# A decoder step with a 32-expert mixture on one core: entry, start and end reordered, expert gates turned by whole-array transposes

## What is computed

```python
x = x + gt1 * _rmsnorm(merged @ w_out, g_post_mix)
h2 = _rmsnorm(x, g_pre_ffn) * (1.0 + sc2) + sh2
logits = h2 @ w_router + b_router            # 32 experts
top_val, top_idx = lax.top_k(logits, 4); gates = softmax(top_val)
# for each expert e: y += gate * swiglu(xb @ w_gate_up[e] + b) @ w_down[e] + b
x = x + gt2 * _rmsnorm(y, g_post_ffn)
```

## Time and profile before

| | before |
|---|---|
| median of 3 runs | 1269.04 us (1268.74 to 1273.98) |
| the profiled execution | 1268.32 us, span 1266.6 us |
| mean granted TensorE clock | 0.946 |
| PE busy | 1087.7 us (86%) |
| DVE busy | 597.7 us (47%) |
| ACT busy | 224.9 us (18%) |
| HBM traffic | 486.16 MB by DMA, mean 384 GB/s |

### The profile page before, as it was taken

How to read it: one execution, slowest core, us unless ns; L and a number is a source line. 1 busy time by engine, 2 the same in 40 slices (tenths; PEclk the granted TensorE clock), 3 DMA queues, 4 the chain that set the end, 5 groups by cost and what they waited for, 6 DMA issues and landing times.

```text
span 1266.6 us, 23750 instructions
## 1 busy us (share of the span) xinstructions
PE 1087.7 (86%) x9790; PEld 462.8 (37%) x9790; DVE 597.7 (47%) x1126; ACT 224.9 (18%) x371; POOL 60.0 (5%) x106
## 2 busy tenths in 40 slices
PE   6999999999888796995788978999866996667996
PEld 3776777784422131331222322333211331112332
DVE  3537744344654352553353643666432552333654
ACT  3002410132311110111011111211111111101112
POOL 0312020310200000000000000000000000000000
PEclk9999999999889898998897999999987998889999
DMA  9979894696899999999999999999999999999996
GB/s 344 306 246 355 316 331 144 212 352 267 321 416 427 428 429 428 428 428 428 428 428 428 426 428 410 394 422 428 428 427 429 427 428 427 428 427 429 428 428 246
DMA packets 67282, 486.16 MB, mean 384 GB/s; under 512 B 6013, under 2 KB 28882, under 8 KB 40426
## 3 DMA queue, kind: packets, MB, share of 16 engines
q1 hardware_dynamic: 59584, 462.11, 88.2%
q0 software_dynamic: 6496, 19.48, 4.7%
q10 hardware_dynamic: 1130, 3.50, 0.8%
HBM read 479.31 MB, written 5.77 MB: 383 GB/s over the span
## 4 chain that ended last, share of the span: by engine, by line
DMA 45%; PE 26%; DVE 1%; issue 0%; ACT 0%; DVEq 0%; ACTq 0%
DMA big<-in_w_down 28%; PE PB L1147 13%; DMA big<-in_w_gate_up 12%; PE PB L1174 7%; DMA hTG<-in_w_down 5%; PE PB L1108 2%; PE PB L1116 2%; PE PB L1132 1%; PE PB L1123 1%; PE PB L1140 0%; PE PB L1093 0%; DVE big L1476 0%; DVE cst L1473 0%; DVE big L1473 0%; ACT L1419 0%
## 5 line engine op out<-in xcount | busy, mean ns | idle before, releaser
L1147 PE MATMUL PB<-big,cst 128*32 128x512 f32 x2768 | 354.3, 655 | 109.5 <-DMA big<-in_w_gate_up 109.5
L2057 DVE TENSOR_TENSOR tok<-PB,cst 32x512 f32<-32x512 f32 x188 | 129.1, 687 | 257.9 <-ACT cst L1418 255.9
L1147 PEld LDWEIGHTS PB<-big,cst 128*32 128x32 f32 x2768 | 88.7, 115 | 346.3 <-issue 182.6
L1174 PE MATMUL PB<-big,cst 128*32 128x512 f32 x1408 | 165.0, 597 | 20.9 <-DMA big<-in_w_down 20.9
L719 PE MATMUL PB<-hTG,big 128*128 128x264 f32 x576 | 138.1, 394 | 1.5 <-DVE hTG L1470 1.5
L2034 DVE TENSOR_SCALAR mod<-PB 64x512 f32<-64x512 f32 x48 | 33.3, 693 | 208.0 <-PE PB L1147 207.9
L719 PEld LDWEIGHTS PB<-hTG,big 128*128 128x128 f32 x576 | 107.8, 192 | 28.9 <-issue 11.8
L1413 ACT ACTIVATE mod<-PB 64x512 f32<-64x512 f32 x48 | 28.4, 592 | 420.4 <-PE PB L1147 420.4
L1108 PE MATMUL PB<-wide,att 128*32 128x256 f32 x1176 | 80.3, 406 | 5.5 <-DVE att L2029 5.5
L1174 PEld LDWEIGHTS PB<-big,cst 128*32 128x32 f32 x1408 | 38.9, 109 | 104.4 <-issue 64.9
L1108 PEld LDWEIGHTS PB<-wide,att 128*32 128x32 f32 x1176 | 39.7, 115 | 61.0 <-issue 36.7
(11 more groups left out here) (346 smaller groups left out, 909.2 us busy)
## 6 DMA issues: line engine op xcount, KB each, us to landing
big<-in_w_gate_up SPq DMA_DIRECT2D x115, 2048.0 KB, 30.9
big<-in_w_down SPq DMA_DIRECT2D x57, 2048.0 KB, 23.7
hTG<-in_w_gate_up SPq DMA_DIRECT2D x13, 2048.0 KB, 38.6
big<-in_w_mod SPq DMA_DIRECT2D x24, 1024.0 KB, 7.6
big<-in_w_in SPq DMA_DIRECT2D x22, 1024.0 KB, 9.0
hTG<-in_w_down SPq DMA_DIRECT2D x6, 2048.0 KB, 24.1
wide<-in_cache_k POOLq DMA_DIRECT2D x16, 256.0 KB, 5.9
big<-in_w_out SPq DMA_DIRECT2D x4, 1024.0 KB, 10.1
```

Source lines behind the costliest of these rows:

```text
L1147: mm = pe.matmul(GU[32 * j:32 * j + 32, :], mo["xT"][:, (2 * u + r) * M:(2 * u + r + 1) * M], groups(w[:, r * 2 * D:(r + 1) * 2 * D])[:, j ...
L1174: mm = pe.matmul(DN[32 * j:32 * j + 32, :], mo["actT"][:, (4 * u + r) * M:(4 * u + r + 1) * M], w[:, r * D + half * 512:r * D + (half + 1) ...
L2057: mm = dve.tensor_tensor(mo["y"][rows, :], DN[rows, :], mo["y_part"][other, :], ALU.add)
```

## The change

1. **Start.** The three loads at the head of SP's queue go to the head of ACT's, so that SP begins with `x_prompt`. Pieces of the shift weights are loaded between the two halves of the first `w_in` unit. PE gets extra matmuls on zeros (`warm`) into a bank that is overwritten, and the order of `x_T`, `scale_part(3)` and `mt0` changes; DVE scales the first seven of eight `hT` chunks before the last is there.
2. **Entry.** `G` and `hT` change places in `hTG`. Units 6 and 9 are loaded in halves: 6's right half right after unit 7, 9's left half after the first half of the last residual. For that the sample rows of `x` are read again by POOL into `xn[:, 1, :]`. The last chunk's scaling is split round the last routing on DVE, POOL's two adds wait for `xT_ready`, and `gather` adds the shift rows itself for the first block. PE gets extra matmuls (`spare`) between steps.
3. **Gates.** `Pg` is written four times side by side by the same reduce, whose input now has a broadcast dimension (128x384 out), and `gates_T` is three whole-array transposes.
4. **End.** The last block is taken out of ACT's loop, so that the Sqrt table is loaded before the last copy. The scatter is done in eight matmuls of 32 rows with a wait after four, prompt before samples; the squares, roots and gains follow that order; chunk 1's rows are scaled and stored in two halves. All four small stores are on SP.

```diff
-AUX_ORDER = ["vt"] + [f"xt{k}" for k in range(KC)] + """
-    mt0 shm mtS ...
+AUX_ORDER = ["vt"] + [f"xt{k}" for k in range(KC - 1)] + ["mt0", f"xt{KC - 1}"] + """
+    shm mtS ...
-        hT = hTG[:, 0:KC * T].rearrange("p (k t) -> p k t", k=KC)
+        hT = hTG[:, 2 * D:2 * D + KC * T].rearrange("p (k t) -> p k t", k=KC)
-        G = hTG[:, KC * T:KC * T + 2 * D].rearrange("p (s n) -> p s n", s=2)
+        G = hTG[:, 0:2 * D].rearrange("p (s n) -> p s n", s=2)
-        mo["Pg"] = cst[:, dead + 512:dead + 608]
+        mo["Pg"] = cst[:, dead + 512:dead + 896]
+        xs_again = xn[:, 1, :]
@@ SP
+            def load_half(n, r):
+                u = n % NU
+                rows = a["w_gate_up"][0, n // NU, u * 2 * P:(u + 1) * 2 * P, :].rearrange("(p r) n -> p r n", r=2)
+                sp.dma_start(unit_slot(n)[:, r * 2 * D:(r + 1) * 2 * D], rows[:, r, :]).then_inc(unit_landed(n)[0], 16)
-            for dst, src in ((vrows[VC:VC + 8, :], a["c_prompt"]...), (vrows[VC + 8:VC + 72, :], a["c_sample"]...),
-                             (cst[:, 0:P + E], a["consts"][:, 0:P + E])):
-                sp.dma_start(dst, src).then_inc(S("small_loaded"), 16)
-                if u == ("in", FIRST, 1):
-                    for i in range(4):
+                if u[0] == "in" and u[1] == FIRST:
+                    for i in range(2 * u[2], 2 * u[2] + 2):
                         sp.dma_start(sh_pieces[:, i, :, :], ...)
             load_unit(7)
+            load_half(6, 1)
             sp.wait_ge(S("wo_half_used"), 1)
             load_unit(4)
             sp.wait_ge(S("yo_full"), 4)
             load_unit(5)
+            sp.wait_ge(S("x1_half"), 2 * NCH - 1)
+            load_half(9, 0)
             sp.wait_ge(S("x_spilled"), 32)
             sp.wait_ge(S("x1_half"), 2 * NCH)
             sp.wait_ge(S("aux_full"), AUX["xa1"] + 1)
-            load_unit(6)
+            load_half(6, 0)
             sp.wait_ge(S("aux_full"), AUX["rt1"] + 1)
-            load_unit(9)
+            load_half(9, 1)
@@ POOL
+            pool.wait_ge(S("aux_full"), AUX["so"] + 1)
+            pool.dma_start(xs_again[0:NS, :], a["x_sample"][:, 0, :]).then_inc(S("ffn_loaded"), 16)
             pool.wait_ge(S("h2_ready"), NCH)
+            pool.wait_ge(S("xT_ready"), 1)
             for lo, hi, row in ffn_shift:
                 pool.tensor_tensor(xn[:, 1, lo:hi], xn[:, 1, lo:hi], row, ALU.add).then_inc(S("h2_ready"), 1)
@@ PE
+            def warm(n):
+                flat = SH1p.rearrange("p k r -> p (k r)")
+                for _ in range(n):
+                    pe.matmul(PB[0][:, 0:256], flat[:, 0:P], flat[:, :], start=True, stop=True)
+            pe.wait_ge(S("zeros_ready"), 1)
+            warm(4)
+            warm(6)
             scale_part(0)
+            warm(3)
             scale_part(1)
             for k in range(4):
                 x_T(k)
             scale_part(2)
-            for k in range(4, KC):
+            for k in range(4, 6):
                 x_T(k)
             scale_part(3)
+            x_T(6)
+            warm(1)
             first_cols("mt0", 1)
+            x_T(7)
+            warm(3)
+            def spare(bank, n):
+                for _ in range(n):
+                    pe.matmul(bank[:, :], zeros[:, :], biases[:, 0:512], start=True, stop=True)
+            spare(GU, 3)          # before x1_T(1); 4 after logits(1), 2 in pos, 3 after the totals
-            def gather():
+            def gather(unshifted=False):
...
+                if unshifted:
+                    for part, (_lo, _hi, row) in enumerate(ffn_shift):
+                        for j in range(4):
+                            by_row = row.rearrange("t (u g i r) -> t g u r i", u=2, g=4, r=2)[:, j]
+                            mm = pe.matmul(MISC[32 * j:32 * j + 32, part * P:(part + 1) * P], mo["Pm"][:, M:2 * M],
+                                           by_row, start=False, stop=(part == 1))
             def gate_up(e, b):
-                    pe.wait_ge(S("xT_ready"), b + 1)
                     pe.wait_ge(S("pgT_ready"), b + 1)
                     # the four bias matmuls
+                    pe.wait_ge(S("xT_ready"), b + 1)
             def gates_T():
                 for c in range(NCH):
                     n = rows_of[c]
-                    for j in range(4):
-                        mm = pe.matmul(GU[32 * j:32 * j + 32, c * P:c * P + n], mo["Pg"][0:n, c * M:(c + 1) * M],
-                                       ident[0:n, 0:n], start=True, stop=True, tile_position=(0, 32 * j))
+                    mm = tr(GU[:, c * P:c * P + n], mo["Pg"][0:n, c * 4 * M:(c + 1) * 4 * M], n)
-            pe.wait_ge(S("h2_ready"), NCH + 2)
-            gather()
+            pe.wait_ge(S("h2_ready"), NCH)
+            gather(unshifted=True)
@@ PE, end (scatter of the last block)
+            for i, (j, c) in enumerate(((0, 0), (2, 0), (1, 1), (3, 1), (1, 0), (3, 0), (0, 1), (2, 1))):
+                if i == 4:
+                    pe.wait_ge(S("totals_full"), 5)
+                rows = slice(32 * j, 32 * j + 32)
+                mm = pe.matmul(acc(c, j // 2), mo["PgT"][rows, c * P:(c + 1) * P], mo["y_part"][rows, :],
+                               start=False, stop=i >= 4, tile_position=(32 * j, 0))
@@ DVE
+            def h2_last(lo, hi, row):
+                stt(xn[:, 1, lo:hi], x1_last[:, lo:hi], sv("rs2", 1, 2), row, ALU.mult, ALU.mult)
+            h2_last(0, 512, attf[:, 0:512])
             read_logits(1)
             route(1)
+            h2_last(512, 768, attf[:, 512:768])
+            h2_last(768, D, C("sbias")[:, 0:256])
-            eqG_sum = mo["eqG"].rearrange("p (c k m) -> p c m k", c=NCH, k=TOPK)
-            Pg3 = mo["Pg"].rearrange("p (c m) -> p c m", c=NCH)
+            eqG_sum = mo["eqG"].rearrange("p (c k m) -> p c m k", c=NCH, k=TOPK).unsqueeze(2).to_broadcast(
+                [P, NCH, 4, M, TOPK])
+            Pg3 = mo["Pg"].rearrange("p (c j m) -> p c j m", c=NCH, j=4)
             top_less(1)
+            dve.wait_ge(S("h2_ready"), NCH + 2)
             do(dve.memset(mo["y"], 0.0), "y_ready")
```

More of the change, by code:

```diff
@@ L481, in _ @@
                 sp.dma_start(g2r[32 * j:32 * j + NS, 1, 0:256], g_rows[1, 1:9, cols]).then_inc(S("g2_loaded"), 16)
-            for j in range(2):
+            for j in range(4):
                 sp.wait_ge(S("final_ready"), 3)
@@ L1073, in _ @@
             logits(1)
+            spare(MISC, 4)
             bank = begin("pos")
@@ L1077, in _ @@
                 for b in blocks:
+                    if b == 1:
+                        spare(MISC, 2)
+                        pe.wait_ge(S("aux_free"), AUX["rt1"] + 1)
+                        zero(ACC2, 256)
                     pe.wait_ge(S("mask_ready"), CHUNKS.index(b) + 1)
@@ L1084, in _ @@
             mm.then_inc(S("totals_full"), 1)
+            spare(MISC, 3)
             def down_biases():
@@ L1108, in gather @@
                         mm = pe.matmul(MISC[32 * j:32 * j + 32, 0:256], mo["Pm"][:, c * M:(c + 1) * M],
-                                       by_row, start=(c == 0), stop=(c == NCH - 1))
+                                       by_row, start=(c == 0), stop=(c == NCH - 1 and not unshifted))
+                if unshifted:
+                    for part, (_lo, _hi, row) in enumerate(ffn_shift):
+                        for j in range(4):
+                            by_row = row.rearrange("t (u g i r) -> t g u r i", u=2, g=4, r=2)[:, j]
+                            mm = pe.matmul(MISC[32 * j:32 * j + 32, part * P:(part + 1) * P], mo["Pm"][:, M:2 * M],
+                                           by_row, start=False, stop=(part == 1))
                 mm.then_inc(S("gathered"), 1)
@@ L1212, in _ @@
             mm.then_inc(S("scattered"), 1)
-            for c in range(2):
-                for half in range(2):
-                    rows = slice(64 * half, 64 * half + 64)
-                    mm = pe.matmul(acc(c, half), mo["PgT"][rows, c * P:(c + 1) * P], mo["y_part"][rows, :],
-                                   start=False, stop=True, tile_position=(64 * half, 0))
-                mm.then_inc(S("scattered"), 1)
-            pe.wait_ge(S("m2_ready"), 1)
+            pe.wait_ge(S("m2_ready"), 5)
             for j in range(4):
@@ L1410, in _, with gated @@
             nblocks = act.value_load(tab[0:1, E:E + 1], min_val=1, max_val=MAXB)
[L1411 removed]
+            before_last = act.value_load(tab[0:1, E + 1:E + 2], min_val=1, max_val=MAXB)
+            def gated(b):
                 act.wait_ge(S("w_used"), b * NU + 4)
@@ L1418, in _, with block_squares @@
                 act.activation(mo["y_part"], DN[:, :], ACT.Copy).then_inc(S("y_copied"), 1)
+            with act.Fori(0, before_last) as b:
+                gated(b)
+                parts(b)
+            gated(before_last)
             do(act.activation(sv("sl"), eps[:, :], ACT.Sqrt))
-            act.wait_ge(S("scattered"), nblocks + 1)
```

(41 more changed lines are left out.)

84 lines of the change are left out of this document (49 added, 35 removed).

## The result

| | before | after |
|---|---|---|
| median, runs of one comparison | 1272.57 us (20 runs, 1267.58 to 1278.94) | 1281.24 us (20 runs, 1278.05 to 1286.95) |
| ratio | | 1.0072, 95% interval 1.0056 to 1.0089 |
| profiled execution, span | 1268.32, 1266.6 us | 1278.05, 1276.4 us |
| mean granted TensorE clock | 0.946 | 0.954 |
| PE, DVE busy | 1087.7, 597.7 us | 1079.8, 699.7 us |

The change makes the kernel 0.7% slower. The forecast was 1268.7 us, with no change as the likeliest outcome. Two things have to be known before profiles are compared. The runs of the kernel before lie mostly in two groups, about 1268 to 1271 and 1273 to 1278 us (in each later set of its runs too), and its profiled execution is of the lower one. The profiled execution after is the lowest of its 20. So the spans differ by 9.8 us, the medians by 8.7.

What follows compares the result with a forecast made beforehand. PE was taken to bound the kernel to about 350 us, then the DMA stream, nearly tied with PE in places. Start -2.5, entry -2.0, first block -0.2, gates +4.4, end 0.0 gave -0.3 us: 1268.7 us, range 1262.5 to 1275.

Steps and rivals of the forecast that it cites:

- -2.5 (start): Start: earlier SP loads 0.5 us, scale_part(3) order 0.5 us, clock 1.5 us gained; bounds 0 and -4.3.
- -2.0 (entry): Path to tab_ready: earlier last routing and gather, less POOL's adds holding DVE; 2.0 us gained, bounds +1.5 and -3.5.
- +4.4 (gates): Expert blocks: longer reduce delays the DMA stream 3.0 us in the long stretch and the end 1.4 us.
- y: Extra time per PE-bound block once DVE closes the loop through the longer reduce; taken as 0.7 us.
- 7y - 1.9: Long stretch after 776.73 us: stream delay at the load waiting for the seventh block; 3.0 us at y = 0.7.
- 2y: End: two blocks behind the last wait for weights each take y longer; 1.4 us.
- pairs against 29.4 us: Long stretch: two blocks take 28.8 us of PE against 29.4 us of DMA per expert, leaving 0.6 us room.
- up to 2 us later: Start: normed rows come no sooner, and up to 2 us later, with small loads beside a full DMA.
- The clock's term: Start: extra matmuls keep PE's clock up through the first matmul passes; 1.5 us gained.
- I cost them at nothing: Entry: half transfers cost 0 us, since all ten units land before SP sees tab_ready.
- Start and entry give nearly nothing: Rival: small loads take back SP's gain, clock falls anyway, gates nearly alone; +3.5 us, 1272.5 us, chance 0.2.
- DVE closes the loop at a higher price: Rival in expert_block: reduce 3.24 us or an unseen wait, y = 1.15; +3.8 us, 1272.8 us, chance 0.15.

Runs made afterwards that it cites:

- e1: The changed kernel with the old gates back (narrow reduce, twelve small matmuls); 1273.13 us, ratio 1.0024 to the kernel before.
- e2: The kernel before with only the gates changed; 1281.61 us, ratio 1.0072 to the kernel before.
- e6: The changed kernel with DVE reducing to 128x96 as before, then writing the four copies with one tensor_copy; 1272.08 us, ratio 0.9993 to the kernel before.
- e15: e7 with the three small loads moved from the head of SP's queue to the head of ACT's; 1272.79 us, ratio 1.0006 to the kernel before.
- e7: The kernel before with only twelve matmuls on zeros added at the start; 1267.51 us, ratio 0.9953 to the kernel before.
- e11: The changed kernel with the b_down loads issued after block 22 and down biases added before expert 24; 1277.94 us, ratio 1.0049 to the kernel before.
- e13: The changed kernel with gates prepared ahead, small loads back on SP, POOL's adds after the tables, b_down loads late; 1265.31 us, ratio 0.9945 to the kernel before.
- e5: The changed kernel with POOL's two adds waiting for tab_ready in place of xT_ready; 1280.35 us, ratio 1.0063 to the kernel before.
- e12: The kernel before with only the end's part of the change; 1268.92 us in one run.
- e4: The changed kernel with DVE preparing the next block's gates before waiting for ACT's copy and adding y; 1271.97 us, ratio 1.0016 to the kernel before.
- e14: The kernel before with the start's matmuls on zeros, new gates prepared a block ahead, b_down loads late; 1267.29 us, ratio 0.9959 to the kernel before.

## Why the prediction was wrong

The sum was -2.5 (start) -2.0 (entry) -0.2 (first block) +4.4 (gates) +0.0 (end). The profiles show +3.0 (start), -1.8 up to `tab_ready` and +1.7 behind it (entry), +6.8 (gates) and 0.0 (end), 9.7 of the 9.8 us. The measured median is 12.5 us above the forecast; 3.5 us of that is the base, which is 1272.57 in 20 runs and was 1269.04 in three.

*Gates: mechanism right, two sizes off.* The reduce was put at 2.77 us and took 2.98 in the steady blocks; the block grew by 0.96 us in place of 0.7. At that y the rule 7y - 1.9 gives 4.8 us for the stream; it lost 3.7 (waits ending at 941.64 against 934.96, less the 3.0 it came in late), and 0.6 us of that was back at 1168.02. The end was put at 2y. It cost 3.7 us (1258.31 - 1168.02 against 1248.52 - 1161.94), because a pair of blocks now takes 30.7 us, more than the DMA's 29.4, so the two pairs ahead of the last two blocks became DVE-bound too. The forecast applied "pairs against 29.4 us" to the stream and forgot it for the end. Together 6.8 us, and 6.7 and 7.9 by L in e1 and e2, in place of 4.4. PE saves 0.22 us a block (e6) in place of 0.35. The lines of the chain behind these waits, two of before and one of after:

```profile
934.96 2.65 PE PB L1147 x16
...
1161.94 1.93 PE PB L1174 x16
...
941.64 1.97 PE PB L1190 x16
```

The Trainium skill ("VectorE: DVE Perf Modes", section "Mode 1× (REGULAR) — the baseline") has one result a cycle whatever the stride, from which the forecast worked out an estimate of 1.75 us for the reduce. The trace disagrees with 2.98, and the strided rows of before were the right guide.

*Start: the failed step.* The forecast let the vectors come "up to 2 us later" and still counted 2.5 us gained. The wait for them ended 6.9 us later, since their price was taken from ACT's issue times and not from how long a small load takes beside a full queue. The moved loads alone cost 5.3 us (e15), and this is the largest miss: +3.0 us in the profile where -2.5 was forecast. The clock's term was too small in the other direction: 1.5 us against 2.2 in the profile and 6 in the ratio (e7), most likely because the forecast had read one profile, of the lower group, though the three runs shown were 1268.74, 1269.04 and 1273.98. Both together are +0.8 us against the median (e15's ratio of 1.0006) and +3.0 against the profiled execution.

*Entry: gain right at `tab_ready`, lost behind it.* -1.8 us there, as forecast (-2.0). "I cost them at nothing" was said of the half transfers; nothing was said of `b_down`. POOL's queue is where its adds stand, and eight DMA issues are behind them: moving the adds behind `xT` moved the loads into the stream. Up to the wait at 777.54 the changed kernel loses 1.7 us behind `tab_ready` (777.54 - 347.79 against 774.58 - 346.57). How much of it the loads are is not settled: taking them away gave 2.2 us in e11 and 0.6 in e13. The adds' hold on DVE was foreseen at 1 to 2 us and is 1.8 (e5).

*End:* 0.0, as forecast (e12).

So of the rivals two came true in part. "Start and entry give nearly nothing" had the small loads beside the full queue take back what SP gained, which is what e15 shows, though they took more. The slower one came true in its mechanism, "DVE closes the loop at a higher price": it wanted y = 1.15 or weak other gains to lose time, and got y = 0.96, no gain at start and entry, and the two more pairs at the end.

## What to carry to other kernels

When a cheap operation gets four times as long, look for the place in the loop where its engine idles before looking for a cheaper form: here 4.1 us of idle stood beside a wait of 0.9 us, and moving the work by one wait made its price nothing (e4). When an instruction moves, list what is issued behind it on its queue: the small DMAs behind POOL's adds cost 0.6 to 2.2 us, about as much as the 1.8 us of the adds. When the few runs shown disagree by 0.4%, a profile may be one of two cases, and a change may pay by making the bad case rare, as e7's 12 close runs suggest.

## What the runs showed of the hardware that was not expected

- A small load on ACT's queue took 1.8 us (before) and 2.2 us (e7) from issue to use with SP's small loads ahead of its large ones, and 6.7 us with SP's megabyte loads issued first (e15).
- PE ran slower than the windows say: 16 matmuls took 1.94 us in e2 and 1.07 in e7, and the granted clock in the records is 1.00 from 10 to 24 us in both.
- Two short DVE operations (SCAN on 128x32, CAST on 1x32) took 1.14 and 1.02 us beside POOL's adds and 0.22 and 0.17 without (e5).
- 0.52 MB in rows of 2 KB, issued by POOL, cost 2.2 us beside the stream by L in e11, 0.6 in e13, and nothing measurable with the old entry (e14).
- A DVE reduce with a broadcast dimension inside, 1536 numbers 32 elements apart, takes 2.98 us; reducing 384 and copying four times takes 1.37 (e6).
